# Filler gate steps of a hybrid decoder layer: three fp32r products on 512-column pieces instead of one fp32 product

## What is computed

```
h     = rms_norm(x)
proj  = h @ w_in                      # columns: q|k|v, r|k|v and low-rank downs, gates (4096)
attn  = sliding_window_attention(q, k, v, sinks)       # 16 heads, window 128, blocks of 128
y     = rwkv7(...)                                     # delta-rule state, 16 heads of 64
merged = sigmoid(gates[:, :2048]) * (attn @ w_branch_a) + sigmoid(gates[:, 2048:]) * (y @ w_branch_b)
x    += merged @ w_out
x    += hierarchical_moe(rms_norm(x))                  # 32 experts, top 2 of one group
```

## Time and profile before

| what | time |
|---|---|
| median of three runs | 1731.72 us (1729.35 to 1732.23) |
| profiled execution, span | 1722.8 us |
| TensorE busy in the span | 1447.0 us |
| ScalarE, GpSimd busy | 408.6, 38.1 us |
| attention (first scores to the end of the last unit) | 79.3 us |
| RWKV, half 0 and half 1 | 109.1 and 102.3 us |

### The profile page before, as it was taken

How to read it: one execution, slowest core, us unless ns; L and a number is a source line. 1 busy time by engine, 2 the same in 40 slices (tenths; PEclk the granted TensorE clock), 3 DMA queues, 4 the chain that set the end, 5 groups by cost and what they waited for, 6 DMA issues and landing times.

```text
span 1722.8 us, 25972 instructions
## 1 busy us (share of the span) xinstructions
PE 1447.0 (84%) x11414; PEld 843.6 (49%) x11414; DVE 703.5 (41%) x1043; ACT 408.6 (24%) x550; POOL 38.1 (2%) x34
## 2 busy tenths in 40 slices
PE   7999999999999999997877686777776876867766
PEld 6888888555646688885232242232322321412322
DVE  6665554547365566543323131222222222322222
ACT  5544444334142344443100000000000000000002
POOL 1000000001102010000000000000000000000000
PEclk9999999999999999999888797898888888888888
DMA  9654466341111393857999999999999999999996
GB/s 348 240 184 158 153 204 216 115 162 57 59 57 62 106 320 127 322 215 269 436 427 432 430 431 432 431 433 431 433 430 434 429 435 429 433 431 434 429 428 288
DMA packets 79544, 529.28 MB, mean 307 GB/s; under 512 B 7616, under 2 KB 9930, under 8 KB 65130
## 3 DMA queue, kind: packets, MB, share of 16 engines
q1 hardware_dynamic: 74624, 514.50, 73.3%
q0 software_dynamic: 2192, 9.35, 1.5%
q10 hardware_dynamic: 2650, 4.26, 0.7%
HBM read 521.80 MB, written 6.29 MB: 307 GB/s over the span
## 4 chain that ended last, share of the span: by engine, by line
PE 50%; DMA 41%; DVE 5%; ACT 2%; issue 1%; DVEq 0%; SPq 0%; ACTq 0%
DMA ring<-in_expert_w_up 12%; DMA ring<-in_expert_w_gate 11%; PE ps L930 10%; DMA ring<-in_expert_w_down 8%; PE ps L563 7%; PE ps L1030 6%; DMA arena<-in_expert_w_up 4%; PE ps L642 4%; DMA arena<-in_expert_w_down 4%; PE ps L624 4%; PE ps L564 4%; PE ps L1150 4%; DMA arena<-in_expert_w_gate 2%; PE ps L526 1%; PE ps L833 1%
## 5 line engine op out<-in xcount | busy, mean ns | idle before, releaser
L2031 DVE TENSOR_TENSOR arena<-arena,ps 128x512 f32<-128x512 f32 x248 | 154.0, 682 | 414.9 <-PE ps L1018 413.9
L1030 PE MATMUL ps<-ring,arena 128*32 128x512 f32 x1024 | 156.0, 762 | 93.8 <-DMA ring<-in_expert_w_gate 57.6
L1030 PE MATMUL ps<-arena 128*32 128x512 f32 x1024 | 145.3, 716 | 78.3 <-DMA arena<-in_expert_w_up 48.3
L563 PE MATMUL ps<-h_both,w_hi 128*128 128x512 f32 x544 | 193.8, 401 | 1.4 <-DVE w_lo L1636 1.4
L564 PE MATMUL ps<-h_both,w_lo 128*128 128x256 f32 x544 | 153.5, 282 | 0.0
L642 PE MATMUL ps<-ring,arena 128*128 128x512 f32 x320 | 150.5, 606 | 0.7 <-issue 0.7
L1030 PEld LDWEIGHTS ps<-ring,arena 128*32 128x32 f32 x1024 | 38.6, 134 | 207.6 <-issue 119.1
L1030 PEld LDWEIGHTS ps<-arena 128*32 128x32 f32 x1024 | 37.0, 127 | 175.9 <-issue 113.8
L563 PEld LDWEIGHTS ps<-h_both,w_hi 128*128 128x128 f32 x544 | 102.9, 189 | 27.2 <-DVE w_lo L1636 1.5
L1739 DVE TENSOR_TENSOR v_lo<-ring,v_hi 128x1024 fp32r<-128x1024 f32 x64 | 78.3, 1225 | 70.2 <-ACT v_hi L1347 69.9
L1150 PE MATMUL ps<-ring,arena 128*32 128x512 f32 x512 | 85.4, 827 | 25.0 <-DMA ring<-in_expert_w_down 15.7
(11 more groups left out here) (302 smaller groups left out, 1947.8 us busy)
## 6 DMA issues: line engine op xcount, KB each, us to landing
ring<-in_w_in SPq DMA_DIRECT2D x34, 2048.0 KB, 7.8
arena<-in_expert_w_gate SPq DMA_DIRECT2D x15, 4096.0 KB, 32.9
ring<-in_expert_w_down SPq DMA_DIRECT2D x15, 4096.0 KB, 33.7
ring<-in_expert_w_gate SPq DMA_DIRECT2D x15, 4096.0 KB, 32.7
arena<-in_expert_w_up SPq DMA_DIRECT2D x15, 4096.0 KB, 32.4
arena<-in_expert_w_down SPq DMA_DIRECT2D x15, 4096.0 KB, 33.4
ring<-in_expert_w_up SPq DMA_DIRECT2D x14, 4096.0 KB, 33.4
ring<-in_w_out SPq DMA_DIRECT2D x8, 2048.0 KB, 8.3
```

What stands on the lines that cost most here:

```text
L563: mm(out, hi[:, 128 * n:128 * n + 128], both(k), start=start and n == 0, stop=False)
L1030: last = mm(ps[32 * c:32 * c + 32, bank, :], XS[:, k, 32 * j:32 * j + 32], w[:, HID * c:HID * c + HID], start=i == 0, stop=i == 3, tile_po ...
L2031: last = v.tensor_tensor(xs, xs, ps[:, banks[nb], :], ALU.add)
```

## The change

Each filler step becomes the three fp32r products. For this the five blocks' weights are split in 80 pieces of 512 columns (`UF = 80`, two steps each, one per token tile) in four buffers `f4`: ScalarE writes `hi` (`f_hi`), GpSimd writes `lo` (`f_lo`). Both go in program order between the other work of their engines. `f_hi(y)` waits until piece `y - 4` has been used. Both token tiles of a block now run together in banks 6 and 7, so a new block's first step waits until ScalarE has emptied the bank of the block before. The counts of steps move: 84 of the 160 now lie in attention, 43 in half 0 and 33 in half 1. `U(7)` to `U(14)` move into ring slots 2 and 3, since `h_both` stays in use; filler chunks take only slots 0 and 1, and the branch weights' chunks 2 and 3 wait for the group norm of half 1.

```diff
+        UF = (8 - GD) * KT
+        FILL_U = ((13, 2, 1), (13, 2, 1), (22, 3, 1), (22, 3, 1))
+        FILL_H = (dict(wl=1, ks=1, vtr=3, bon=12, l=3, mt=1, v1=(1, 1, 1, 1, 1), ua=2, s=1, yy=6, end=7),
+                  dict(wl=1, ks=1, vtr=3, bon=10, l=3, mt=1, v1=(1, 1, 1, 1, 1), ua=2, s=1, yy=5, end=0))
+        def pieces_after(key):
+            return min(UF, FILLS[key][1] // 2 + 4)
...
+            def gate_mm(key):                      # TensorE
+                for m in range(*FILLS[key]):
+                    y, t = divmod(m, TT)
+                    b, k = divmod(y, KT)
+                    if t == 0:
+                        pe.wait_ge(S("w_lo"), F0 + y + 1)
+                    if k == 0 and b:
+                        pe.wait_ge(S("gate_out"), 2 * (GD + b - 1) + t + 1)
+                    for p, (w, v) in enumerate(PRODUCTS):
+                        last = mm(ps[:, 6 + t, :], hf(v, k, 128 * t, 128), f_pieces(y)[w],
+                                  start=k == 0 and p == 0, stop=k == KT - 1 and p == 2)
+                    if t:
+                        last.then_inc(S("w_used"), 1)
...
+            def f_lo(upto):                        # GpSimd
+                for y in range(f_at[0], max(upto, f_at[0])):
+                    hi, lo = f_pieces(y)
+                    pool.wait_ge(S("w_hi"), F0 + y + 1)
+                    pool.tensor_tensor(lo, f_src(y), hi.bitcast(F32), ALU.subtract).then_inc(S("w_lo"), 1)
...
+            def f_hi(upto):                        # ScalarE
+                for y in range(f_at[0], max(upto, f_at[0])):
+                    if y % 8 == 0:
+                        act.wait_ge(S(f"slot_full{slot_of(NF + y // 8)}"), landed_by(NF + y // 8))
+                    if y >= 4:
+                        act.wait_ge(S("w_used"), 4 + F0 + y - 3)
+                    f(f_pieces(y)[0], f_src(y), ACT.Copy).then_inc(S("w_hi"), 1)
+            act.wait_ge(S("h_lo_done"), 8)         # behind the low-rank activations
+            f_hi(4)
             for u in range(4):
-                if u:
+                if u == 2:
                     gate_out()
+                    gate_out()
+                if u == 3:
+                    f_hi(2 * KT + 4)
+                    gate_out()
+                    gate_out()
+                f_hi(pieces_after((u, "sc")) - (3, 3, 5, 5)[u])
                 act.wait_ge(S("sm_done"), u + 1)
                 f(probs[:, :, 0:w], probs[:, :, 0:w], ACT.Exp).then_inc(S("ex_done"), 1)
                 f(aes[:, :], aes[:, :], ACT.Exp).then_inc(S("ex_done"), 1)
+                f_hi(pieces_after((u, "sc")))
...
                 f(U(7), U(6), ACT.Square).then_inc(S("sq_done"), 1)
+                f_hi(pieces_after((f"h{hh}", "wl")))
+                if hh == 1:
+                    gate_out()
+                    gate_out()
                 act.wait_ge(S("half_ps"), half_at("ks", hh))
                 f(U(11)..., ACT.Sqrt).then_inc(S("nrm_done"), 1)
...
                 byhead(blocks(U(7), 64), 2, "vt2_done")
-                gate_out()
+                if hh == 0:
+                    f_hi(3 * KT + 4)
+                    gate_out()
+                    gate_out()
```

More of the change, by code:

```diff
@@ L177, in hybrid_layer @@
             h_hi, h_lo = (h2[:, :, x, :] for x in range(2))
+        with ExitStack() as mid:
+            f4 = [over(mid, f"f_{x}", [P, 4, 512]) for x in ("hi", "lo")]
         with ExitStack() as late:
@@ L385, in _ @@
                 load(NL + h, slot(NL + h, LORA_W), cols(LORA0, h, LORA_W))
-            for c in range(16):
+            for c in range(2 * GD):
                 load(NG + c, slot(NG + c), cols(GA0 + 512 * (c // 2), c % 2, 512))
+            for c in range(2 * GD, 16):
+                n = NG + c
+                sp.wait_ge(*((S("chunk_used"), NF - 1 + n - NF) if n < NF + 2 else (S("w_lo"), F0 + 8 * (n - 1 - NF))))
+                sp.dma_start(ring[:, slot_of(n), :].rearrange("p (k n) -> p k n", k=8), cols(GA0 + 512 * (c // 2), c % 2, 512))\
+                    .then_inc(S(f"slot_full{slot_of(n)}"), 16)
             wa = a["w_branch_a"][0].rearrange("(k p) n -> p k n", p=P)
@@ L390, in _ @@
             for c in range(8):
-                load(NM + c, slot(NM + c), (wa, wb)[c % 2][:, :, 512 * (c // 2):512 * (c // 2) + 512])
+                if c == 2:
+                    sp.wait_ge(S("yc_done"), HALVES)
+                sp.wait_ge(*((S("w_lo"), F0 + UF - 8 + 8 * min(c, 1)) if c < 4 else (S("chunk_used"), NF + c - 3)))
+                sp.dma_start(ring[:, c % RING, :].rearrange("p (k n) -> p k n", k=8),
+                             (wa, wb)[c % 2][:, :, 512 * (c // 2):512 * (c // 2) + 512]).then_inc(S(f"slot_full{c % RING}"), 16)
                 if c == 4:
@@ L499, in _ @@
                                        tile16(C("lvlT", 64, 64 * lv)), ALU.mult).then_inc(S("ltm_done"), 1)
+                    f_lo(pieces_after((f"h{hh}", "mt" if lv == 1 else f"v{lv - 1}")))
+            f_lo(UF)
             pool.wait_ge(S("m_lo_done"), 3)
@@ L816, in _ @@
                             last.then_inc(S("v1_ps"), 1)
-                    gate_mm(2 if lv == 1 else 1)
+                    gate_mm((f"h{hh}", f"v{lv}"))
                     if lv == 1:
@@ L920, in _ @@
                 last.then_inc(S("half_ps"), 1)
-                if hh == 0:
-                    gate_mm(8)
-            assert gate_part[0] == 16 * KT
+                gate_mm((f"h{hh}", "end"))
             def late_unit(left, buf, bank, ks, start, stop):
@@ L1427, in _ @@
                 f(gn[:, 1, :], gn[:, 1, :], ACT.Sqrt).then_inc(S("gsd_done"), 1)
-                if hh == 0:
+                f_hi(pieces_after((f"h{hh}", "end")))
+                if hh == 1:
+                    act.wait_ge(S("w_used"), 4 + F0 + UF)
                     gate_out()
-                else:
-                    act.wait_ge(S("chunk_used"), NG + 16)
                     f(m_hi[:, 8:16, :], attnT, ACT.Copy).then_inc(S("m_hi_done"), 1)
```

110 lines of the change are left out of this document (65 added, 45 removed).

## The result

| | before | after |
|---|---|---|
| median of the runs, us | 1731.51 (4 runs, 1729.35 to 1732.23) | 1770.24 (4 runs, 1769.12 to 1774.9) |
| profiled execution, span, us | 1722.8 | 1773.1 |
| ratio after / before, 95% interval | | 1.0249 [1.0226, 1.0273] |

The change makes the kernel 2.5% slower. The prediction had the sign and missed the size: 1741 with a range of 1718 to 1758. The profiled executions differ by 50.3 us, more than the ratio's 43: the change's was the longest of its four, and that of before was a short one.

A forecast was written before the change was run, and what follows sets the result against it. It took the stretch before the untouched, DMA-bound experts as only partly PE-bound. Terms: -14.5 + 6.0 + 3.4 + 5.3 + 2.2 + 2.0 + 3.0 + 2.0 = +9.4 us; span 1732.2, median 1741, range 1718 to 1758.

The forecast's parts named there:

- All in one stretch: Only first scores to first branch product, 304.95 to 595.66 us, counts; the experts' 922.8 us are not touched.
- Unit 0: Attention's first unit: first filler at 310.3 instead of 306.04, exponentials at 317.2 instead of 310.89; cost 6.0 us.
- Units 2 and 3: Attention: copies and sigmoids of new blocks delay exponentials to 13.2 and 15.2 us in; costs 3.4 and 5.3 us.
- Unit 1: Attention: copy 14 waits for piece 10, ready about when VectorE is, no new table load; cost 0.
- All five terms for ScalarE's order: Copies and sigmoids in ScalarE's queue: units 0, 2, 3 cost 6.0, 3.4, 5.3 us; halves 0, 1 cost 2.2, 2.0.
- The shared port: GpSimd subtracts against VectorE products of two SBUF arrays, in attention and halves: 3.0 us, 25 at worst.
- the chain is unchanged: Attention, steps after the scores: 8.8 or 15.0 us match VectorE's chain, which stays as long, so they are hidden.
- The gain of 14.5: Shorter or removed fillers: lone ones 8.5, end of half 0 2.3, small ones 1.5, attention 2.2 us.
- lone fillers without a wait behind them: Halves, after levels 2 and 3 and two state products: eight go, 1.06 us each, gaining 8.5 us.
- rival B: In the bursts a piece takes GpSimd 1.67 us against PE's 1.36: 15 us beyond the forecast, 1756; chance 0.14.
- The clock: PE's four or five new waits lower its clock, up to 1.4 us each: 2 us taken, bounds 0 and 7.
- The base: Whole kernel: profiled span 1722.8 us, with the runs' median 8.9 us over it; forecast span 1732.2 becomes 1741.

The follow-up runs named there:

- e7: Changed kernel with plain fp32 filler steps; ScalarE's 80 copies run beside them, used by nobody, without GpSimd's subtracts: 1754.76 us, 1.0160 of the kernel before.
- e9: Changed kernel, order only: first four copies earlier, fewer copies ahead of exponentials in units 2 and 3, second branch's first load held back: 1753.07 us, ratio 1.0170.
- e3: Changed kernel with the first four fp32r copies ahead of the last gate sigmoids and low-rank activations: 1768.86 us, 1.0231 of the kernel before.
- e6: Changed kernel with plain fp32 filler steps; ScalarE's copies and GpSimd's subtracts run beside them, used by nobody: 1765.27 us, 1.0215 of the kernel before.
- e1: Changed kernel with GpSimd subtracting only 64 of 512 columns from the fifth piece on: 1749.38 us, 1.0109 of the kernel before.
- e4: Changed kernel with plain fp32 filler steps, no copies or subtracts; counts, ring slots, arrays and hand-overs as changed: 1743.66 us, 1.0078 of the kernel before.
- e5: e4 with the numbers of filler steps put back to those of the kernel before: 1738.16 us, 1.0066 of the kernel before.
- e11: Kernel before with three lone filler steps in each half's tail joined to the group of two behind the inverse: 1736.42 us, ratio 1.0056.
- e12: e11 with one 2 MB load held until half 1's last product of 64x64 blocks is done: 1732.37 us, 1.0019 of the kernel before.

## Why the prediction was wrong

- **All in one stretch**, the rest untouched: right.
- **Unit 0** (+6.0; first filler at 310.3, exponentials at 317.2): the unit began 1.5 us later than before, so the first filler at 311.80 is the forecast to the tenth. The size was low: the exponentials ran at 320.70, 2.0 later than that, and the unit took 10.6 us more.
- **Units 2 and 3** (+3.4, +5.3; exponentials 13.2 and 15.2 us in): 13.7 and 17.3 in, the units 7.4 and 9.9 longer. **Unit 1** (0): 3.2 longer. The order is confirmed, `gate_out` in unit 3 to a tenth (2.8 for 2.7). All five terms for ScalarE's order add up to 18.9; e7 has 14 for the copies, e9 mends 14. This size was about right in sum; it wasn't tested term by term.
- **The shared port** (3.0, bounds 0 and 25): this term failed, and with it the step "the chain is unchanged" by which the fillers after the scores were called hidden. The direction that no row had shown exists, each conflict costs 0.87 to 1.1 us even to an 8-column instruction (4.7 once, in e3), five VectorE lines of a unit meet it and not two, and the reciprocal's chain in half 1 pays 5.2 us (four products and a copy). e6 has 9.5 us for it beside plain steps, e1 24 beside the shorter ones. I had announced the growing chain as a rival, but rival B prices only GpSimd's pace (1.67 us a piece; the mean was 1.56), at 0.14, and PE's waits for pieces are 0.7 us beyond the first. So nothing in the forecast priced what happened.
- **The gain of 14.5**: this failed too, in its largest part, the 8.5 us for "lone fillers without a wait behind them". e4 has that part and about 1 us at the end of half 0 (the other gains need the shorter step), and sixteen more steps of 0.86 in attention: 13.8 - 9.5 = 4.3 over before by my terms, and 14 measured. So some 10 us were not there. It is not that the steps' own time didn't come back: from e5 to e4 it does, 9.1 us. But with them went what they did where they stood. e11 shows it: three steps of each half moved by a few microseconds cost 10 us, as idle in which PE waits for instructions and as a load that starts earlier. An idle that the fillers hid was not in any row, and I took its absence for a proof. The moves of arrays and chunks, which I put at nothing, are in e4 and e5 too; alone they were not tested.
- **The clock** (2.0, bounds 0 and 7): not isolated. Behind most of the long waits PE ran at 1.2 GHz: sixteen transposes took 3.67 us at 372.93, behind 2.98 us, and 1.97 at the full clock. But the eight at 326.20, behind 2.72 us, took 1.06, as at the full clock. These transposes and L840 alone lost 3.2 us; how much of such time lies on the path stays open.
- **The base**: I took the 8.9 us from the span to the runs' median for launch and end. In every run since, the time is the span and 1.8 us; the profiled execution of before was simply a short one. The forecast is not touched by it: 1741 is the runs' median and 9.4 us.

By sizes, with the ratio's 43 us against the 9.4 of my sum: 34 us are missing. Some 10 are gain that was not there and 21 the subtracts (24 for 3.0), 31 together; the rest is not placed, and the lower clock is in both and was not taken apart. The range failed at its upper end: with the port at its own bound of 25 us the sum gives 1763, above the 1758 where the range ended, and the loss of the gain came on top.

## What to carry to other kernels

A filler that keeps PE busy is worth what it takes only if nothing else hides under it; before counting it as a cost, move one or take one away and look. Work handed to GpSimd beside a VectorE chain of SBUF-to-SBUF products should be priced at one whole GpSimd instruction of this size on each of them, small ones included, and at more where GpSimd has a run of them ready (4.86 us for 0.17 in e3). An in-order engine that both feeds the fillers and carries the chain should do the chain's work first, and give back only buffers that are free by then.

## What was not expected

- Five GpSimd subtracts of 512 columns beside four VectorE products of 1024 and a copy alternate one by one: 2.03 us each for 1.27 alone, and 2.17 to 2.32 for 1.22 on VectorE. A copy of 16 columns took 1.23 us there; without subtracts (e7) the same copy takes 0.17.
- Holding back one 2 MB load gave 6 us by the ratios (e11 against e12). Beside that load PE had stood 3.58 us, until a late packet of its instructions was in, with the lower clock behind it (0.93 and 0.90 in the two 10 us that follow 570).
- A table load costs nothing where ScalarE has nothing to do ahead of a sigmoid, and 1.28 us of PE's wait where copies stand ahead of it: e4, with the same hand-over, shows no wait of PE for the bank, e7 shows 3.7 us in attention.
